# Written-out repetitions of a hybrid pooling and gated DeltaNet kernel put into hardware loops

## The reference, cut to what matters

```python
h = concatenate([meta_tokens, x])                    # 16 + 512 tokens, 2048 channels
proj = rmsnorm(h, norm_w) @ w_in                     # 2048 x (2*1024 + 4*2048 + 2*16 + 2*2048)
u_pool, z_pool, q, k, v, z_dn, b, a, gate_pool, gate_dn = split(proj)
y_pool = (trailing_means(u_pool, windows 2/4/8/16) - u_pool) @ pool_mix * scale * silu(z_pool)
q, k, v = silu(causal_conv4(q, k, v)); q, k = l2norm(q), l2norm(k)
o = chunk_gated_delta_rule(q, k, v, sigmoid(b), -exp(A_log) * softplus(a + dt_bias))   # 16 heads of 128
y_dn = rmsnorm(o, dn_norm_w) * silu(z_dn)
merged = sigmoid(gate_pool) * (y_pool @ w_pool_out) + sigmoid(gate_dn) * (y_dn @ w_dn_out)
out = rmsnorm((h + merged @ w_o)[16:], final_norm_w)
```

## Time and profile before

| | |
|---|---|
| time, median of 3 runs | 1936.51 us (1932.39 to 1937.05) |
| profiled execution, its own time | 1936.51 us |
| its span | 1934.8 us |
| instructions with busy time | 38055 |
| PE busy | 1848.5 us, 96% |
| DVE busy | 1313.6 us, 68% |
| ACT busy | 1003.7 us, 52% |
| DMA queue q8, instructions | 114 packets, 1.87 MB |
| DMA queue q14, instructions | 52 packets, 0.42 MB |

### The profile page before, as it was taken

One profiled execution on the slowest core, in us unless ns is written; L12 is line 12 of the kernel. 1 busy time (PEld: TensorE's weight loads), 2 busy tenths in 40 slices (PEclk: granted clock), 3 DMA queues, 4 the chain that ended last, 5 costly groups with the idle time before them and its releaser, 6 DMA issues.

```text
span 1934.8 us, 38055 instructions
## 1 busy us (share of the span) xinstructions
PE 1848.5 (96%) x15265; PEld 1732.9 (90%) x15265; DVE 1313.6 (68%) x2420; ACT 1003.7 (52%) x2316; POOL 125.6 (6%) x158
## 2 busy tenths in 40 slices
PE   5889999999999999999999999999999999999998
PEld 4889899989999999989999998999999788888886
DVE  7868758768787786868878687777777544335332
ACT  5444445757566665756667576645456322224232
POOL 2000010101001010100101011000000000000000
PEclk8999999999999999999999999999999999999999
DMA  4323464536555463644536365365644534347202
GB/s 148 99 66 111 110 175 125 145 89 191 137 147 135 131 166 101 189 134 144 143 116 172 108 187 137 92 186 170 173 118 140 188 113 140 117 135 289 101 22 87
DMA packets 311000, 264.90 MB, mean 137 GB/s; under 512 B 12202, under 2 KB 266627, under 8 KB 310179
## 3 DMA queue, kind: packets, MB, share of 16 engines
q1 hardware_dynamic: 284018, 197.35, 35.5%
q0 software_dynamic: 12992, 39.57, 7.5%
q10 hardware_dynamic: 13824, 25.70, 3.7%
HBM read 221.03 MB, written 42.60 MB: 136 GB/s over the span
## 4 chain that ended last, share of the span: by engine, by line
PE 63%; DVE 17%; ACT 7%; issue 6%; DMA 6%; POOL 1%; SPq 0%; ACTq 0%; DVEq 0%; POOLq 0%
PE pj L887 32%; PE pj L818 17%; PE pg L818 8%; DVE wl L1746 4%; ACT wh L1212 3%; PE pt L818 2%; DVE stg L2095 2%; DMA st<-gram_scratch 2%; DVE raw L1779 1%; PE pj L844 1%; DVE st L2150 1%; DVE st L2147 1%; DMA raw<-in_w_in 1%; DMA dec<-in_consts 1%; DVE raw L1762 1%
## 5 line engine op out<-in xcount | busy, mean ns | idle before, releaser
L887 PE MATMUL pj<-xh,wh 128*128 128x256 f32 (+2 forms) x2688 | 788.1, 293 | 43.3 <-DVE wl L1746 15.7
L887 PE MATMUL pj<-xl,wh 128*128 128x256 f32 (+2 forms) x2688 | 762.1, 284 | 0.0
L887 PE MATMUL pj<-xh,wl 128*128 128x256 f32 (+2 forms) x2688 | 761.7, 283 | 0.0
L1746 DVE TENSOR_TENSOR wl<-raw,wh 128x512 fp32r<-128x512 f32 x752 | 506.3, 688 | 299.3 <-ACT wh L1212 292.9
L1212 ACT ACTIVATE wh<-raw 128x512 fp32r<-128x512 f32 x752 | 458.6, 626 | 425.4 <-PE pj L887 195.8
L887 PEld LDWEIGHTS pj<-xh,wh 128*128 128x128 f32 x2688 | 511.2, 190 | 55.0 <-ACT snap L1212 17.6
L887 PEld LDWEIGHTS pj<-xl,wh 128*128 128x128 f32 x2688 | 512.1, 191 | 1.0 <-issue 1.0
L887 PEld LDWEIGHTS pj<-xh,wl 128*128 128x128 f32 x2688 | 510.8, 190 | 0.0
L1212 ACT ACTIVATE bwh<-rawb 128x256 fp32r<-128x256 f32 x192 | 64.9, 405 | 174.3 <-PE pj L818 168.8
L844 PE MATMUL pj<-xh,wh 128*128 128x260 f32 (+1 forms) x512 | 147.3, 288 | 3.4 <-ACT xin L1212 2.8
L818 PE MATMUL pj<-yh,bwh 128*128 128x512 f32 x384 | 150.1, 391 | 0.3 <-DVE yl L2299 0.3
(11 more groups left out here) (301 smaller groups left out, 2432.0 us busy)
## 6 DMA issues: line engine op xcount, KB each, us to landing
raw<-in_w_in SPq DMA_DIRECT2D x224, 512.0 KB, 4.7
head_scratch<-stg ACTq DMA_DIRECT2D x64, 264.0 KB, 3.8
rawb<-in_w_dn_out SPq DMA_DIRECT2D x16, 1024.0 KB, 6.1
rawb<-in_w_o SPq DMA_DIRECT2D x12, 1024.0 KB, 5.5
kq<-head_scratch SPq DMA_DIRECT2D x8, 1056.0 KB, 9.8
gates_scratch<-stg ACTq DMA_DIRECT2D x32, 256.0 KB, 2.0
rawb<-in_w_pool_out SPq DMA_DIRECT2D x8, 1024.0 KB, 5.5
yraw<-branch_scratch SPq DMA_DIRECT2D x6, 1024.0 KB, 7.9
```

The lines of the kernel that those rows point to most:

```text
L887: mm = pe.matmul(bank[:, c0:TH], w[:, slot, k, :], xx[what][:, kt, c0:TH], start=opens and one and kt == 0, stop=closes and last and kt == ...
L1746: tt(wl[:, slot, :, :], raw[:, buffer_of(of, par, what), HK * half:HK * (half + 1), :], wh[:, slot, :, :].bitcast(F32), ALU.subtract).then ...
```

## The change

Seven Python loops that wrote a body out once for each iteration become hardware loops (`Fori`), whose body stands once in the code and is repeated by a branch:

- TensorE: the pooling group 2 (one iteration), the pairs 1 to 6 (six iterations), the gate blocks 4 to 13, two a turn (five iterations);
- ScalarE: the pooling groups 2 and 3 (two), the pairs 1 to 7 (seven), the same gate blocks (five);
- VectorE: the pairs 1 to 7 (seven), the same gate blocks (five).

In these bodies the block number is an `Of(...)`, so the compared counts and a few addresses come out of registers.

```diff
--- before.py
+++ after.py
@@ -968,7 +968,7 @@
 
             pool_blocks(0, False, "u")
             pool_blocks(1, True, "u")
-            for g in range(2, GROUPS - 1):
+            with pe.Fori(2, GROUPS - 1) as g:
                 pool_blocks(g, False, "u")
             pool_blocks(GROUPS - 1, False, "k")
 
@@ -1130,7 +1130,7 @@
                     block_products(pair_at(p, k), k % 2, PAIR_KINDS[k], (PAIR_KINDS + (kind_after,))[k + 1], hook)
 
             pair_blocks(0, None, "k")
-            for p in range(1, PAIRS - 1):
+            with pe.Fori(1, PAIRS - 1) as p:
                 pair_blocks(p, p - 1, "k")
             pair_blocks(PAIRS - 1, PAIRS - 2, "gate")
 
@@ -1140,9 +1140,9 @@
                     if m is not None:
                         delta(PAIRS - 1, m)
                 block_products(CP_GATE0 + k, k % 2, "gate", "gate", last_pair)
-            for i in range(2, NGATE // 2 - 1):
+            with pe.Fori(2, NGATE // 2 - 1) as i:
                 for k in range(2):
-                    block_products(CP_GATE0 + k + 2 * i, k, "gate", "gate", no_hook)
+                    block_products(Of(i, 2, CP_GATE0 + k), k, "gate", "gate", no_hook)
             for k in range(2):
                 block_products(NCP - 2 + k, k, "gate", "gate", no_hook)
 
@@ -1372,7 +1372,7 @@
 
             pool_blocks(0, True, False)
             pool_blocks(1, False, True)
-            for g in range(2, GROUPS):
+            with act.Fori(2, GROUPS) as g:
                 pool_blocks(g, False, False)
 
             def first_tap(p, k, c):
@@ -1566,7 +1566,7 @@
                         block_acts(b, k % 2, PAIR_KINDS[k], ("q", "v", "z", "k")[k], event, hook)
 
             pair_blocks(0, None)
-            for p in range(1, PAIRS):
+            with act.Fori(1, PAIRS) as p:
                 pair_blocks(p, p - 1)
 
             def gate_store(i, c):
@@ -1603,9 +1603,9 @@
                     else:
                         gate_tail(CP_GATE0 + k - 1, 1 - k % 2, t)
                 gate_block(CP_GATE0 + k, k % 2, before, last_pair)
-            for i in range(2, NGATE // 2 - 1):
+            with act.Fori(2, NGATE // 2 - 1) as i:
                 for k in range(2):
-                    gate_block(CP_GATE0 + k + 2 * i, k, lambda t, k=k: gate_tail(CP_GATE0 + k - 1 + 2 * i, 1 - k, t), no_hook)
+                    gate_block(Of(i, 2, CP_GATE0 + k), k, lambda t, k=k: gate_tail(Of(i, 2, CP_GATE0 + k - 1), 1 - k, t), no_hook)
             gate_block(NCP - 2, 0, lambda t: gate_tail(NCP - 3, 1, t), no_hook)
 
             def split_b(jp, j, q):
@@ -2263,7 +2263,7 @@
                     steps(b, k % 2, PAIR_KINDS[k], [tile_of(p, k, c) for c in range(2)], lambda c, k=k: tile_free(p, k, c), event, hook, early)
 
             pair_blocks(0, None)
-            for p in range(1, PAIRS):
+            with dve.Fori(1, PAIRS) as p:
                 pair_blocks(p, p - 1)
 
             def no_event(t):
@@ -2283,9 +2283,9 @@
                     if m is not None:
                         delta(PAIRS - 1, m)
                 gate_block(CP_GATE0 + k, k % 2, (lambda t: z_first(PAIRS - 1, CP_GATE0) if t == 1 else None) if k == 0 else no_event, last_pair)
-            for i in range(2, NGATE // 2 - 1):
+            with dve.Fori(2, NGATE // 2 - 1) as i:
                 for k in range(2):
-                    gate_block(CP_GATE0 + k + 2 * i, k, no_event, no_hook)
+                    gate_block(Of(i, 2, CP_GATE0 + k), k, no_event, no_hook)
             gate_block(NCP - 2, 0, no_event, no_hook)
 
             def split_b(jp, j, q):
```

## The result

The changed kernel takes 1965.47 us (median of 4 runs, 1962.09 to 1971.3) against 1936.78 in the same session (4 runs, 1932.39 to 1937.26): a ratio of 1.0156 with a 95% interval of 1.0126 to 1.0187, slower by 28.7 us. The forecast had the sign, the range (1932 to 1966) and the likely place, but a size of 9 us, a third of what came. Its profiled execution took 1964.96 us, with a span of 1963.3.

The account below looks back on a forecast made before the run. The prediction took TensorE to bound the kernel, busy 1848.5 of 1934.8 us. TensorE reloads 5.0, ScalarE's edges 1.5 and register instructions 2.5 gave +9.0 us on 1936.51, so 1945.5 us, range 1932 to 1966.

Parts of the forecast that it names:

- Branches at 0: At all loop edges: a branch whose code is at hand costs 0, as in stage B's existing loops.
- the gate body kept: TensorE's four gate edges: the 44 KB body repeats without loading, 0 us, with 11.6 us as the high end.
- The pair body loaded again in every turn: TensorE's pair loop: the 147 KB body is not kept, so code loads at five edges, +5.0 us.
- VectorE's edge at 0: VectorE's pair-loop edge: a reload of 2.4 us is covered and 26 us of idle a pair absorb the backlog, 0.
- The length of a load: At an edge: 1.8 us transfer start plus packet time of 1.1 (TensorE) or 0.6 (others), so 2.9 and 2.4 us.
- q8 was to stay at 9 packets a pair: Sign in the looped pairs: TensorE's code queue moves as many packets as before, 9 a pair, and fewer in the gate stretch.
- the sum with the gate edges loaded too (1949.5): Alternative by the skill's fetch rule: the gate body also reloads, 9.0 + 4 x 1.0 us, total 1949.5.
- I take 1.0 us, nearer to 0: TensorE's five pair edges: each reload shows 1.0 us of an estimated 2.9, so +5.0 us, ends 0 and 14.5.
- rows 7: Profile rows from 1600 to 1700 us in stage B: PE busy 100.00 of 100.00 us across three edges of TensorE's loop.
- The rival of full reloads (1977): TensorE stands 2.9 us at nine edges, ScalarE and VectorE add 2.4 at six: 40.5 us; chance 0.15.
- ScalarE's slack: ScalarE's six pair edges: 1.9 us slack at `snap` against a 2.4 us reload; 0.25 us each, +1.5, ends 0 and 3.
- Registers: Seven pairs: register instructions lengthen about half of six late TensorE waits by 0.12 us, 0.35 a pair, +2.5, ends 0 and 5.

Follow-up runs that it names:

- five against two edges: Only TensorE's pair loop made a loop, against the kernel before: one pair a turn, five back edges, 1964.08 us; two pairs a turn, two back edges, 1947.50 us.
- the hint: An added instruction at the pair loop's head naming the back edge's target for early fetching; on all three engines of the changed kernel, 1945.88 us, ratio 1.0050.

## Why the prediction was right or wrong

**Right.** Branches at 0 and the gate body kept: the gate and pool loops alone cost nothing (1.0002). The pair body loaded again in every turn: q8 at 114 packets. Five edges of TensorE and six of ScalarE as the places. VectorE's edge at 0: its loop added to ScalarE's changes nothing that can be told. The length of a load was estimated well in its sum, 2.9 us for TensorE and 2.4 for the others; stands of 2.36 to 3.00 and 2.3 us were found. The parts were luck: 1.8 us ahead of the packet and 1.1 for it were counted, where the packet starts within 0.4 us and 1.6 to 1.8 us pass behind its end.

**Signs.** q8 was to stay at 9 packets a pair. It has 11 in each of the four windows from 460.27 to 937.17 us, which the unchanged total of 114 hides. The gate stretch has fewer, as forecast, so the sum with the gate edges loaded too (1949.5) was larger for a load that did not happen.

**The step that failed** is "I take 1.0 us, nearer to 0, since at the edges of rows 7 TensorE ran on through the branch". Those edges had their code at hand, so they bear on a jump, not on a load; the packet came only as TensorE finished its last products, nothing issued ahead covered it, and TensorE stood 2.7 us. The term also lacked what follows a stand, 1.5 us and more lost at the lower clock. Measured, an edge is 4.8 us (five against two edges), or 4.1 by the kernel with TensorE's loop alone, without and with the hint ((25.9 - 5.6) / 5). That is 20 to 24 us in place of 5.0, above even the term's high end of 14.5. The rival of full reloads (1977) had the right stand at the pair edges, but counted gate edges that cost nothing, let ScalarE's and VectorE's loads add 14.4 us where they mostly overlap, and lacked the clock as well; its total was 11.5 us too high.

**ScalarE's slack.** The prediction read 1.9 us at the `snap` copy, and a reload of 2.4 us to show 0.5. At that copy it was right: 0.30 us at the one uncovered edge. But it followed ScalarE no further than the high parts behind the copy. ScalarE had no idle time before its next deadline, `ktok`, 7 us on, where the slack in the kernel before was 0.05 us and TensorE now waited 1.77 us. In the loops of ScalarE alone that is 18 us for six edges with its registers, where +1.5 was forecast. In the full change most of this hides under TensorE's own stands: taking all loads of ScalarE and VectorE away brought 4 us (30 - 26), in intervals of 5 to 6 us either side.

**Registers.** +2.5 us forecast, +7.8 measured (4.5 to 10.9). Counting late waits left out TensorE's own instructions, with which alone the kernel was 5.6 us longer, and that behind a wait of 1.74 us or more the clock can fall.

**The sum again,** from the runs: 20 us for the loads of all engines (30 - 10) and 8 to 10 us of registers.

## What to carry to other kernels

A loop whose body is loaded again pays at each back edge on the engine that sets the time, in full: price it as the length of a load plus what the clock loses behind a stand, and ask whether the target can be called ahead. Read the queues of code by stretch: the equal totals here hid more loads in one stage and fewer in another. A slack at one deadline of an engine is not its slack: follow the engine to the next ones before a backlog is called absorbed. Edges that happen on all engines at once overlap, so removing one engine's share shows less than it costs alone.

## What the runs showed of the hardware

- TensorE stood 2.36 to 3.00 us at a back edge to code that had to be loaded, ScalarE 2.3 us on average; a body of two gate blocks (44 KB) and one of four (86 KB) repeated without a gap, the latter with no q8 packet between 1330 and 1420 us.
- At the five edges of the changed kernel and the five of the kernel with TensorE's loop alone, TensorE went on 1.6 to 1.9 us after the end of the q8 packet at the edge.
- A hint given some 114 us ahead of the jump took TensorE's whole stand away, though 11 packets of its code start in that pair (574.19 to 688.54 us). On ScalarE and VectorE, whose bodies have 18 and 21 KB, the code was no longer loaded in each turn: q14 moved 6 packets over seven pairs in place of 68.
- Behind the same wait for `xin` the granted clock stayed at 1.00 up to 1.72 us and was down at 0.50 from 2.24 us on; between these both were seen.
